# Two four-branch attention blocks in one kernel: latent projections regrouped by kind, stage boundaries done by token tiles, layer 1's memory keys made between the layers

## The chip, the cores and the metric

The kernel runs on one core of one Trainium2 chip. The metric is the device time of one execution in microseconds (us). Engines: TensorE (PE) with its weight loads (PEld), VectorE (DVE), ScalarE (ACT), GpSimd (POOL), SyncE (SP).

## The reference

One sequence of 512 tokens of width 1024 goes through two blocks of two layers each, all in float32.

A layer of the first block projects x by `w_in` into a latent query (384), a latent key and value (256), a rotated key (32), queries, keys and values of a stick-breaking and of a forgetting attention (256 each), four forget columns, memory queries (256), four gates (256 each) and a merge input (128). Each of four branches has four heads:

```python
q  = (rms(c_q) @ w_qb).reshape(b, s, 4, 96)        # 64 plain + 32 rotated
kv = (rms(c_kv) @ w_kvb).reshape(b, s, 4, 128)     # 64 key + 64 value
log_f = log_sigmoid(fox_f + fox_bias); c = cumsum(log_f)   # fox: logits + c[t] - c[s]
mk, mv = split(mem @ w_mem_kv)                      # mem has 256 rows
for n in range(4):
    yb = branches[n] * silu(gate_z[:, :, n])
    merged += sigmoid(merge_r @ w_merge_up)[:, :, n] * (yb @ w_branch[n])
x = layer_norm(ALPHA * x + merged @ w_out)
```

The branches are mla (causal, with the latents), sb (stick breaking), fox (causal with decay) and mem (over `mem`). A layer of the second block applies an rms norm, projects, runs four attentions A (dense), B (window), C (neighbourhood) and D (difference of two softmaxes), multiplies each by `silu` of a gate and adds the output projection to x. A last rms norm ends it.

## The kernel before, in words

**Precision.** Every projection is done in float32 by three matmuls of a rounded part (`xh`, `wh`) and a rest (`xl`, `wl`): lines 1338 to 1340, once for each of the contracted tiles of 128 (`k`). Weights come by DMA from SP into `wr`, two in flight, ScalarE rounds them (line 1480) and VectorE and GpSimd in turn subtract (lines 1805, 2245), 512 columns at a time; such a piece is a step `cast`. A projection lies "feature-major" (weights stationary, 512 tokens moving) or by token tiles (128 tokens stationary, 256 columns moving).

**Order.** `plan` (line 296) writes one list of steps, and each engine's program walks the same list and takes its own part, so the list fixes the order on each engine. All engines work strictly in that order; waits are on semaphores. Banks and buffers are taken and given back in the plan. In each attention stage `alongside` (line 528) interleaves the attention (main), the next branch's projections (fill) and the end of the branch before (tail), by modelled costs (`cost_of`, line 240; a lead of 5000 ns of fill, `LEAD`). `tick` (line 331) places one due cast, and in the beginning one step of the rope tables (`first_tables`, line 775), at fixed places between pieces of matmul. `wnext` takes the next weight and first lays down all of its casts that are still due.

**First block.** The features of x (transposes on PE, line 1297, rounding on ScalarE, rest on VectorE, line 1812) are made for all four token tiles. Then come the memory query, the gate of the memory branch and `project_mem` (line 606), which makes the memory keys and values of both layers; those of layer 1 are stored and loaded back later (`mkvstore`, `mkreload`). The stages are mem (filled by `mla_proj`, line 626), mla (filled by the sb projections and the split of the four forget columns), sb (filled by `fox_proj`, line 726: fox gate, forget columns, forget gate, fox projections) and fox (filled by three quarters of the merge). `mla_proj` makes the latents, their norms, four 96-wide query heads, each turned by its own rope step (line 1435; line 1921 copies it from the bank), four 64-wide key heads, the values and the gate. An mla logit is one matmul over 96 rows for each head. The forget gate is three functions on ScalarE, a sum along the tokens and eight copies on VectorE.

**Between layers.** The last quarter of the merge runs for eight tiles, each ends in a step `merged` (lines 1620, 1995). Output weights follow, four of 256 columns, each for four token tiles; the first matmul waits for merged tile 7 (`act_ready`, line 1231). With the last weight the norm of a token tile begins (`norm_x`: statistics, root on ScalarE, a Newton step, an Identity on ScalarE, the gain on VectorE, the bias on GpSimd, line 2280), then in layer 1 an rms norm, then the transposes of the next features. All features come before the next projection.

**Second block.** A's projections come alone; then stages A, B, D, C, filled by the next projections and by `out_partial` (line 931). Each query and key is turned by a `rope2` (line 1442) right behind its projection (`behind`, line 892). D's output is normed (line 1450). A gate takes two banks, a sigmoid each on ScalarE and a product each on VectorE (line 1891):

```python
held.append((yield from gemm("fm", w, 128 * c, 128 * c + 128, ("x", ep), range(8))))
...
put("gate", l=l, br=br, u=u, banks=held)
give(*held)
```

ScalarE's functions lie in table sets; a step whose function isn't in the set at hand gets a load ahead of it (`FUNCTIONS`, line 292).

Of the kernel before, what the change touches and what calls it, by code (L numbers as in the profile page):

```python
# [14 lines left out]
P = 128  # L15
S = 512
# [11 lines left out]
LEAD = 5000  # L28
# [6 lines left out]
def constants():  # L35
# [16 lines left out]
    col = np.zeros((P, 1), np.float32)  # L52
    col[64:96, 0] = np.concatenate([invf, invf])
    put("invf", col)
# [152 lines left out]


# [31 lines left out]
def cost_of(s):  # L240

    k = s.kind
    if k == "mm":
        n = s["n"] if s["mode"] in ("fm", "fox", "up", "br") else s["c1"] - s["c0"] if s["mode"] != "kvv" else 256
        return len(s["ks"]) * 3 * n * 0.451
# [15 lines left out]
def weights_in_order():  # L261

    out = []
    for l in range(2):
        for name, c0, n in (("mq", 2212, 256), ("g3", 3236, 256)):
            out.append((name, 8, n, l, c0))
        if l == 0:
            out += [(f"mkv{j}{n}", 8, 256, j, 256 * n) for j in (1, 0) for n in range(2)]
        out += [("cq0", 8, 256, l, 0), ("cq1", 8, 256, l, 256), ("ckr", 8, 160, l, 512), ("qb", 3, 384, l, 0),
                ("kvb", 2, 512, l, 0), ("g0", 8, 256, l, 2468)]  # L270
# [21 lines left out]
FUNCTIONS = {"gate": (GATES,), "sqk": (GATES,), "qk": (LOGS, TANHS), "dqk": (LOGS, TANHS), "mtanh": (TANHS,)}  # L292
# [3 lines left out]
def plan(known):  # L296
# [20 lines left out]
    st = {"i": 0, "split": 0, "load": 0}  # L317
# [37 lines left out]
    def pieces(ks, **at):  # L355
        for k in range(len(ks)):
            put("mm", ks=ks[k:k + 1], k0=ks[0], first=at["start"] and k == 0, last=k + 1 >= len(ks), done=False, **at)
# [5 lines left out]
    def gemm(mode, j, c0, c1, act, ks, n=S, tile=0, b=None, off=0, start=True):  # L363
        if b is None:
            b = GR[0].take()
        yield from pieces(ks, start=start, mode=mode, j=j, c0=c0, c1=c1, act=act, n=n, tile=tile, b=b, off=off)
        return b

# [21 lines left out]
    def gate(name, ep, br, l):  # L390
        w = wnext(name)
        held = []
        for c in range(2):
            held.append((yield from gemm("fm", w, 128 * c, 128 * c + 128, ("x", ep), range(8))))
            if c == 0:
                yield
        u = U.take()
        put("gate", l=l, br=br, u=u, banks=held)
        give(*held)
# [11 lines left out]
    def attention(l, br, front, finish):  # L411
# [60 lines left out]
        while later:  # L472
            yield 0
# [132 lines left out]
    def project_mem():  # L606
        for i in range(2):
            run(features("mem", i, X0))
        give(*X0)
        for j in (1, 0):  # L610
            for n in range(2):
                tm = TM.take() if j else None
                w = wnext(f"mkv{j}{n}")
                for c in range(2):
                    if n == 0:
                        b = drain(gemm("fm", w, 128 * c, 128 * c + 128, ("mem",), range(8), n=256))
                    else:
                        b = drain(gemm("tok", w, 0, 256, ("mem",), range(8), tile=c))
                    put("mkv", j=j, n=n, c=c, b=b, tm=tm)
                    give(b)  # L620
                wdone(w)
                if tm:
                    put("mkvstore", n=n, tm=tm)
                    give(tm)

    def mla_proj(l, box):
# [40 lines left out]
        b = yield from gemm("fm", w, 64, 160, ("x", l), range(8))  # L667
# [5 lines left out]
        yield  # L673
        w = wnext("qb")
        held = None
        for h in range(5):
            if h < 4:
                b = yield from gemm("fm", w, 96 * h, 96 * h + 96, ("nq", l), range(3))
                tm = TM.take()
                put("qb", l=l, h=h, b=b, tm=tm)  # L680
                give(b)
# [1763 lines left out]
```

## Time and profile before

| | |
|---|---|
| median of 3 runs | 1636.21 us (1634.75 to 1637.97) |
| profiled execution | 1632.88 us |
| its span, first to last instruction | 1631.1 us |
| mean granted TensorE clock | 0.950 of full |
| busy: PE, PEld, DVE, ACT, POOL | 1449.6, 1104.7, 924.1, 711.6, 370.7 us |

The span is the profiled execution without what lies around it, 1.8 us. Busy times of one engine are those of all its instructions, those that overlap counted once. A row of the timeline gives the start in us from the span's start, the length, and in brackets the idle time of the engine ahead of it with what ended it. L1338 is line 1338 of the kernel before.

### The profile page before, as it was taken

What the parts mean: (1) busy time and instruction counts of PE and PEld (TensorE: products, weight loads), DVE (VectorE), ACT (ScalarE), POOL (GpSimd) and SP (SyncE); (2) the same over time, 40 slices, a digit from 0 to 9 for tenths busy, and PEclk for the clock granted to TensorE, in tenths of its full rate; (3) what the DMA queues carried; (4) which work ended last, traced back from release to release, by engine and by line L of the source; (5) the groups of instructions that cost most, each with busy time, mean ns of one, the idle gap of its engine ahead of it and who ended that gap; (6) DMA issues with size and microseconds to landing.
All of it is one profiled execution on the core that took longest, in us unless ns stands there. A gap on an engine that the chain in (4) does not pass through costs nothing.

```text
span 1631.1 us, 21032 instructions
## 1 busy us (share of the span) xinstructions
PE 1449.6 (89%) x7904; PEld 1104.7 (68%) x7904; DVE 924.1 (57%) x1729; ACT 711.6 (44%) x1501; POOL 370.7 (23%) x269
## 2 busy tenths in 40 slices
PE   6898997999879989979989599998799799997897
PEld 5864784777867657757769466665578666664676
DVE  4547436556562563474674855467645565558555
ACT  2543544465333435444552535345333434445343
POOL 1313121245222221212461311320001111310001
PEclk8999998999989999989999699999899899998999
DMA  6552220124321121201254232521032423411221
GB/s 211 149 113 61 82 79 26 43 69 161 104 104 43 53 78 52 79 13 45 68 185 104 78 65 65 98 80 37 30 113 69 126 52 65 110 52 46 75 75 52
DMA packets 178152, 130.93 MB, mean 80 GB/s; under 512 B 76964, under 2 KB 167460, under 8 KB 178052
## 3 DMA queue, kind: packets, MB, share of 16 engines
q1 hardware_dynamic: 167126, 113.60, 24.2%
q10 hardware_dynamic: 10926, 15.99, 3.2%
q8 instruction: 63, 1.03, 0.3%
q14 instruction: 37, 0.30, 0.1%
HBM read 116.72 MB, written 12.85 MB: 79 GB/s over the span
## 4 chain that ended last, share of the span: by engine, by line
PE 72%; DVE 16%; ACT 6%; issue 3%; DMA 1%; ACTq 1%; SPq 0%; DVEq 0%
PE pb L1338 18%; PE pb L1339 17%; PE pb L1340 17%; PE pb L1362 6%; PE pb L1411 6%; PE pb L1389 4%; ACT prob L1467 2%; ACT tmp L1467 2%; DVE small L2078 1%; PE pb L1442 1%; DVE xl L1812 1%; DVE prob L2091 1%; PE pb L1373 1%; DVE scr L2100 1%; DMA wr<-w_out 1%
## 5 line engine op out<-in xcount | busy, mean ns | idle before, releaser
L2245 POOL TENSOR_TENSOR wl<-wr,wh 128x512 fp32r<-128x512 f32 x168 | 226.2, 1346 | 932.4 <-ACT wh L1480 927.5
L1338 PE MATMUL pb<-xh,wl 128*128 128x512 f32 (+1 forms) x784 | 339.8, 433 | 25.4 <-DVE wl L1805 9.2
L1339 PE MATMUL pb<-xl,wh 128*128 128x512 f32 (+1 forms) x784 | 312.0, 398 | 0.0
L1340 PE MATMUL pb<-xh,wh 128*128 128x512 f32 (+1 forms) x784 | 311.7, 398 | 0.0
L1480 ACT CAST wh<-wr 128x512 fp32r<-128x512 f32 x368 | 209.2, 600 | 116.0 <-PE pb L1340 76.4
L1805 DVE TENSOR_TENSOR wl<-wr,wh 128x512 fp32r<-128x512 f32 x200 | 156.5, 785 | 120.7 <-ACT wh L1480 119.9
L1338 PEld LDWEIGHTS pb<-xh,wl 128*128 128x128 f32 (+1 forms) x784 | 150.7, 192 | 99.1 <-issue 53.7
L1340 PEld LDWEIGHTS pb<-xh,wh 128*128 128x128 f32 (+1 forms) x784 | 150.2, 192 | 34.7
L1339 PEld LDWEIGHTS pb<-xl,wh 128*128 128x128 f32 (+1 forms) x784 | 151.1, 193 | 29.0 <-issue 3.8
L1389 PE MATMUL pb<-cst,prob 128*128 128x128 f32 x768 | 120.5, 278 | 37.8 <-DVE prob L2106 24.7
L1338 PE MATMUL pb<-wh,xl 128*128 128x256 f32 x448 | 133.6, 298 | 18.4 <-issue 12.9
L1389 PEld LDWEIGHTS pb<-cst,prob 128*128 128x128 f32 x768 | 94.8, 143 | 70.7 <-issue 33.7
L1339 PE MATMUL pb<-wl,xh 128*128 128x256 f32 x448 | 130.4, 291 | 0.0
L1340 PE MATMUL pb<-wh,xh 128*128 128x256 f32 x448 | 130.0, 290 | 0.0
L1467 ACT ACTIVATE prob<-prob,small 128x512 f32<-128x512 f32 (+3 forms) x128 | 76.3, 597 | 123.1 <-DVE small L2055 122.8
L1467 ACT ACTIVATE prob<-pb,small 128x512 f32<-128x512 f32 (+1 forms) x96 | 58.6, 613 | 136.3 <-DVE small L2042 86.3
L1467 ACT ACTIVATE tmp<-pb,cst 128x512 f32<-128x512 f32 (+3 forms) x116 | 74.5, 642 | 95.8 <-DVE tmp L2146 26.9
L1338 PEld LDWEIGHTS pb<-wh,xl 128*128 128x128 f32 x448 | 89.6, 200 | 21.9 <-issue 15.2
L2114 DVE COPY prob<-pb 128x512 f32<-128x512 f32 (+3 forms) x128 | 70.9, 554 | 46.4 <-PE pb L1389 45.1
L1699 ACT COPY prob<-pb 128x512 f32<-128x512 f32 (+3 forms) x128 | 61.2, 478 | 80.3 <-PE pb L1389 80.2
L1339 PEld LDWEIGHTS pb<-wl,xh 128*128 128x128 f32 x448 | 89.8, 200 | 1.0 <-issue 0.9
L1340 PEld LDWEIGHTS pb<-wh,xh 128*128 128x128 f32 x448 | 89.6, 200 | 0.0
(206 smaller groups left out, 2593.0 us busy)
## 6 DMA issues: line engine op xcount, KB each, us to landing
wr<-w_in SPq DMA_DIRECT2D x40, 1024.0 KB, 5.1
wr<-w_in SPq DMA_DIRECT2D x48, 256.0 KB, 4.5
wr<-w_out SPq DMA_DIRECT2D x10, 1024.0 KB, 5.1
wr<-w_branch SPq DMA_DIRECT2D x48, 128.0 KB, 2.3
x<-prob SPq DMA_DIRECT2D x12, 512.0 KB, 2.6
wr<-w_out SPq DMA_DIRECT2D x48, 128.0 KB, 2.9
wr<-w_mem_kv SPq DMA_DIRECT2D x4, 1024.0 KB, 9.9
prob<-x ACTq DMA_DIRECT2D x2, 2048.0 KB, 8.0
```

Of the source, the lines that this page charges most:

```text
L1338: e.matmul(ps, ll, rh, start=start, stop=False)
L1339: e.matmul(ps, lh, rl, start=False, stop=False)
L1340: t = e.matmul(ps, lh, rh, start=False, stop=stop)
L1362: t = e.matmul(bank(b)[:, 0:128 * (hi - lo)], lhs, rhs, start=True, stop=True)
L1389: t = e.transpose(bank(b)[:, c], probs(p)[:, c], C("ident"))
L1411: t = e.matmul(bank(b)[64 * half:64 * half + 64, lo:hi], v_[:, j, vc:vc + 64], turns(s["t"][half])[:, j, lo - 256 * ih:hi - 256 * ih], sta ...
L1467: return e.activation(o, i, f, bias=C("zero", 0, i.shape[0]) if bias is None else bias, scale=scale, **kw)
L1480: e.copy(wh[:, j % 2, c0:c1], wr[:, j % 2, c0:c1]).then_inc(w_hi.sem, w_hi.mark((j, c)))
L1699: t = e.copy(turns(t_)[:, lo:hi, 128 * i:128 * i + 128], bank(b)[:, 0:128 * (hi - lo)].rearrange("p (j c) -> p j c", c=128))
L1805: t = e.tensor_tensor(wl[:, j % 2, c0:c1], wr[:, j % 2, c0:c1], wh[:, j % 2, c0:c1].bitcast(F32), ALU.subtract)
L2114: t = e.tensor_copy(turns(t_)[:, lo:hi, 128 * i:128 * i + 128], bank(b)[:, 0:128 * (hi - lo)].rearrange("p (j c) -> p j c", c=128))
L2245: t = e.tensor_tensor(wl[:, j % 2, c0:c1], wr[:, j % 2, c0:c1], wh[:, j % 2, c0:c1].bitcast(F32), ALU.subtract)
```

## The change

- The weights `ckr`, `qb` and `kvb` are loaded in narrow pieces that put columns of a kind together: the latent's last tile, then the forget columns twice beside the rotated key twice; the plain parts of the four heads in two tiles, the rotated parts in one; keys in two tiles, then values. The forget columns' own weights, matmuls and buffers go. Positions are turned once for the key and once for all four query heads. A logit is two matmuls, over 64 plain and over 32 rotated rows.
- The forget gate moves from the sb stage to the end of `mla_proj`, its copies between the fox projections; the mla gate moves ahead of the queries.
- Gates use tanh of half the input, one bank at a time; the factor 1/2 goes into later products.
- `project_mem` makes one layer's memory keys; layer 1's are made behind the last output weights of layer 0 from a second load of `mem`.
- Output weights: the first begins with six of eight merged tiles for four token tiles, the last two are taken together token tile by token tile, with the norm's steps (now two products on VectorE with mean and root) and the next features between them; casts are held back meanwhile.
- The first projection (layer 0's memory query, A's gate) is done for 256 tokens, then the other two token tiles' features, then the other 256.
- In A and B and D `behind` waits three pieces; `out_partial` starts with four of six inputs for two tiles, ahead of the end of the D stage's tail; `LEAD` is 4500. At the start, x and mem are issued from ScalarE's queue and the rope tables begin behind the memory query.

```diff
-LEAD = 5000
+LEAD = 4500
...
-FUNCTIONS = {"gate": (GATES,), "sqk": (GATES,), "qk": (LOGS, TANHS), "dqk": (LOGS, TANHS), "mtanh": (TANHS,)}
+FUNCTIONS = {"gate": (TANHS, GATES), "sqk": (GATES,), "qk": (LOGS, TANHS), "dqk": (LOGS, TANHS), "mtanh": (TANHS, GATES)}
...
-        if due:
+        if due and not st["hold"]:
...
+    def opened(w, ep, between):
+
+        held = [GR[0].take() for _ in range(2)]
+        for half in range(2):
+            for c in range(2):
+                drain(gemm("fm", w, 128 * c, 128 * c + 128, ("x", ep), range(8), n=256, b=held[c], off=256 * half,
+                           end=half == 1))
+            if not half:
+                between()
+        return held
...
-        b = yield from gemm("fm", w, 64, 160, ("x", l), range(8))
+        b = yield from gemm("fm", w, 128, 256, ("x", l), range(8))
         put("krope", l=l, b=b)
...
         w = wnext("qb")
...
+        for c in range(2):
+            b = yield from gemm("fm", w, 128 * c, 128 * c + 128, ("nq", l), range(3))
+            put("qnope", l=l, c=c, b=b)
             give(b)
             tick()
             yield
...
+        turn_rope("k", None)
+        yield
+        w = wnext("kvb")
+        for c in range(2):
+            b = yield from gemm("fm", w, 128 * c, 128 * c + 128, ("nkv", l), range(2))
+            put("knope", l=l, c=c, b=b)
...
+        turn_rope("q", tm)
...
         wdone(w)
-        for x in gate("g0", l, "mla", l):
-            if x is not None:
-                box["u"] = x
-            yield
+        e_ = TM.take()
+        put("foxgate", l=l, e=e_)
+        give(e_)
...
-        b = yield from gemm("fox", -1, 0, 36, ("x", l), range(8))
...
+        w = wnext("wo")
+        held = [drain(gemm("tok", w, 0, 256, ("m", l), range(6), tile=i, end=False, stop=False)) for i in range(4)]
+        for i in range(4):
+            out_tile(0, i, drain(gemm("tok", w, 0, 256, ("m", l), (6, 7), tile=i, b=held[i], start=False)))
...
+        pair = [wnext("wo") for _ in range(2)]
+        st["hold"], late = True, []
+        for i in range(4):
+            for m in (2, 3):
+                b = drain(gemm("tok", pair[m - 2], 0, 256, ("m", l), range(8), tile=i))
+                advance_late(late)
+                out_tile(m, i, b)
...
+            parts = mem_parts(1)
+            for turned in ((0, 1), (2,), (3,), ()):
+                next(parts)
+                advance_late(late)
+                for i in turned:
+                    run(features(1, i, (X[i],)))
...
         def behind(n, tm, sq):
+            for _ in range(3):
+                yield
...
+        at = {"ckr": [(0, 512, 128), (128, 2208, 32), (160, 2208, 32), (192, 640, 32), (224, 640, 32)],
+              "qb": [(64 * h, 96 * h, 64) for h in range(4)] + [(256 + 32 * h, 96 * h + 64, 32) for h in range(4)],
+              "kvb": [(64 * h + 256 * r, 128 * h + 64 * r, 64) for r in range(2) for h in range(4)]}
...
+                if br == "mla":
+                    for half, b in enumerate(s["b"]):
+                        r = slice(64 + 32 * half, 96 + 32 * half)
+                        t = e.matmul(bank(b)[:, 0:128 * (hi - lo)], q_rope[r, c, ti], k_rope[r, tk], start=False, stop=True,
+                                     tile_position=(64 + 32 * half, 0))
...
-                    w.wait_ge(a_fn, a_fn.at(("lnapplied", l, i)))
-                    w.wait_ge(d_res, d_res.at(("ln", l)))
-                    e.tensor_tensor(x, x, lnp[:, 0, :], ALU.mult).then_inc(v_fn.sem, v_fn.mark(("lngain", l, i)))
...
+                t = e.scalar_tensor_tensor(x, x, 1.0, bank(b), ALU.add, ALU.mult)
+                t.then_inc(v_fn.sem, v_fn.mark(("gate", s["u"], c), ends=(b,)))
```

## Rows read from the trace of the kernel before

**Rows 1.** The page: busy time; the chain that ended last.
```profile
PE 1449.6 (89%) x7904; PEld 1104.7 (68%) x7904; DVE 924.1 (57%) x1729; ACT 711.6 (44%) x1501; POOL 370.7 (23%) x269
...
PE 72%; DVE 16%; ACT 6%; issue 3%; DMA 1%; ACTq 1%; SPq 0%; DVEq 0%
```

**Rows 2.** Stretches: length, busy us of PE, PEld, DVE, ACT, POOL; PEclk, DMA.
```profile
11.30:20.60 9.30, 0.10 (x2) 0.09 (x1) 5.99 (x9) 5.07 (x10) 5.27 (x4) 0.65 0.51 122
133.90:144.30 10.40, 4.67 (x16) 2.05 (x17) 10.27 (x15) 2.78 (x9) 4.57 (x3) 0.81 0.01 2
266.80:277.30 10.50, 1.21 (x6) 0.82 (x6) 10.19 (x17) 2.37 (x7) 1.40 (x1) 0.66 0.00 0
415.20:421.70 6.50, 0.10 (x2) 0.05 (x1) 6.30 (x9) 3.70 (x7) 3.17 (x2) 0.89 0.11 32
470.30:490.60 20.30, 7.09 (x34) 5.62 (x33) 17.99 (x27) 8.76 (x16) 7.01 (x3) 0.61 0.27 107
907.10:933.80 26.70, 7.92 (x34) 6.32 (x33) 25.47 (x47) 16.21 (x32) 7.02 (x3) 0.59 0.20 81
1273.50:1287.30 13.80, 5.12 (x26) 4.07 (x25) 13.33 (x25) 10.39 (x23) 2.38 (x2) 0.63 0.43 153
961.10:979.30 18.20, 14.37 (x55) 9.86 (x55) 14.78 (x22) 7.03 (x12) 2.60 (x2) 1.00 0.29 59
1114.80:1118.50 3.70, 0.17 (x2) 0.09 (x1) 1.52 (x3) 3.39 (x5) 1.26 (x1) 1.00 0.06 12
1175.90:1195.00 19.10, 13.15 (x80) 10.91 (x79) 10.43 (x18) 4.97 (x8) 1.27 (x1) 0.82 0.44 152
```

**Rows 3.** The same columns, sum of the 18 stretches at half clock.
```profile
sum 162.90, PE 94.25 PEld 72.21 DVE 119.29 ACT 65.76 POOL 38.28; mean PE 5.24 PEld 4.01 DVE 6.63 ACT 3.65 POOL 2.13
```

**Rows 4.** PE's timeline: start, length, line, operation, tiles, shapes.
```profile
24.44 0.40 PE L1338 MATMUL pb<-xh,wl 128*128 128x512 f32 x1
...
43.96 0.39 PE L1340 MATMUL pb<-xh,wh 128*128 128x512 f32 x1
...
903.01 0.28 PE L1338 MATMUL pb<-wh,xl 128*128 128x256 f32 x1
...
903.37 0.28 PE L1338 MATMUL pb<-wh,xl 128*128 128x256 f32 x1
```

**Rows 5.** PE's groups by line and form (count, busy us, mean ns, idle before).
```profile
L1338 PE MATMUL pb<-xh,fwl 128*36 128x512 f32 x16 | 6.5, 405 | 0.0
...
L1338 PE MATMUL pb<-yh,wl 128*64 128x512 f32 x16 | 7.7, 483 | 0.0
...
L1338 PE MATMUL pb<-yh,wl 128*96 128x512 f32 x24 | 11.1, 463 | 1.9 <-DVE tmp L1930 1.5 <-issue 0.4
...
L1435 PE MATMUL pb<-tmp,cst 96*96 96x512 f32 x16 | 9.9, 700 | 7.4 <-DVE tmp L1921 7.4
```

**Rows 6.** PE's timeline: logits over 96 rows, and over 32.
```profile
216.40 1.98 PE L1362 MATMUL pb<-setA 96*128 96x512 f32 x4
...
1105.28 1.14 PE L1373 MATMUL pb<-setA 32*128 32x512 f32 x8
1106.35 0.50 PE L1338 MATMUL pb<-xh,wl 128*128 128x512 f32 x1
1106.69 0.40 PE L1339 MATMUL pb<-xl,wh 128*128 128x512 f32 x1
```

**Rows 7.** Timelines of PE at the start and ScalarE in the stick-breaking stage.
```profile
20.54 0.77 PE L1338 MATMUL pb<-xh,wl 128*128 128x512 f32 x1 [9.20 <-DVE wl L1805]
...
263.00 2.23 ACT L1467 ACTIVATE tmp<-tmp,cst 36x512 f32<-36x512 f32 x3
```

**Rows 8.** PE's groups: the transposes of probabilities.
```profile
L1389 PE MATMUL pb<-cst,prob 128*128 128x128 f32 x768 | 120.5, 278 | 37.8 <-DVE prob L2106 24.7 <-ACT prob L1467 11.9 <-DVE scr L2124 1.2
```

**Rows 9.** DMA issues: queue, count, KB each, median us to landing.
```profile
wr<-w_in SPq DMA_DIRECT2D x48, 256.0 KB, 4.5
...
tmp<-w_in SPq DMA_DIRECT2D x4, 16.0 KB, 3.8
```

More of the change, by code:

```diff
@@ L353, in wdone, with pieces @@
         last.a["done"] = True
-    def pieces(ks, **at):
+    def pieces(ks, end, stop, **at):
         for k in range(len(ks)):
-            put("mm", ks=ks[k:k + 1], k0=ks[0], first=at["start"] and k == 0, last=k + 1 >= len(ks), done=False, **at)
+            over = k + 1 >= len(ks)
+            put("mm", ks=ks[k:k + 1], k0=ks[0], first=at["start"] and k == 0, last=end and over, stop=stop and over,
+                done=False, **at)
             if k + 1 < len(ks):
@@ L361, in pieces, with gemm, advance_late @@
                 yield
-    def gemm(mode, j, c0, c1, act, ks, n=S, tile=0, b=None, off=0, start=True):
+    def gemm(mode, j, c0, c1, act, ks, n=S, tile=0, b=None, off=0, start=True, end=True, stop=True):
         if b is None:
             b = GR[0].take()
-        yield from pieces(ks, start=start, mode=mode, j=j, c0=c0, c1=c1, act=act, n=n, tile=tile, b=b, off=off)
+        yield from pieces(ks, end, stop, start=start, mode=mode, j=j, c0=c0, c1=c1, act=act, n=n, tile=tile, b=b, off=off)
         return b
+    def advance_late(late):
+        return [g for g in late if next(g, g) is not g]
+    def opened(w, ep, between):
[7 more added lines that the diff above has]
+        return held
     def drain(g):
@@ L472, in attention @@
         while later:
-            yield 0
+            yield now() + 2500
             advance()
@@ L779, in first_tables @@
                 yield
-    aside.append(first_tables())
     for l in range(2):
-        run(proj_fm("mq", l, "mem", "q", l, False))
+        w = wnext("mq")
+        if l:
+            held = [drain(gemm("fm", w, 128 * c, 128 * c + 128, ("x", l), range(8))) for c in range(2)]
+        else:
+            held = opened(w, l, lambda: last_features(l, *X))
+        wdone(w)
+        for c in range(2):
+            put("head", l=l, br="mem", part="q", c=c, b=held[c], wide=False)
+        give(*held)
+        if l == 0:
+            aside.append(first_tables())
         u = run(gate("g3", l, "mem", l))
         if l == 0:
-            project_mem()
+            mem_features(0)
+            rest_of(mem_parts(0))
             put("lambdas")
@@ new lines, in plan @@
+        st["hold"] = False
+        if l:
+            for i in range(2):
+                advance_late(late)
+                run(features(2, i))
+            while advance_late(late):
+                pass
+            give(*X, *X0)
+        else:
+            parts = mem_parts(1)
+            for turned in ((0, 1), (2,), (3,), ()):
+                next(parts)
+                advance_late(late)
+                for i in turned:
+                    run(features(1, i, (X[i],)))
+            rest_of(parts)
+            give(*X)
@@ L929, in project, with out_partial @@
         yield
-    def out_partial(l):
+    def out_partial(l, before):
         for m in range(4):
             w = wnext("wo2a")
+            held = {}
+            if m == 0:
+                for i in range(2):
+                    held[i] = yield from gemm("tok", w, 0, 256, ("y2", l), range(4), tile=i, end=False, stop=False)
+                rest_of(before)
             for i in range(4):
-                b = yield from gemm("tok", w, 0, 256, ("y2", l), range(6), tile=i)
+                b = yield from gemm("tok", w, 0, 256, ("y2", l), range(4 if i in held else 0, 6), tile=i, b=held.get(i),
+                                    start=i not in held)
                 put("acc", l=l, m=m, i=i, b=b)
```

553 lines of the change are left out of this document (241 added, 312 removed).

## The prediction

> **What bounds the kernel now.** I read five views, in this order. First the page: TensorE (PE) is busy for 89% of the span, and 72% of the chain that ended last is PE's own work, 16% VectorE's, 6% ScalarE's [rows 1]. The kernel is bound by its matmuls and, where they stop, by short chains on VectorE and ScalarE. So two kinds of edit pay: fewer matmuls, and work for PE in the holes. The holes are 1631.1 - 1449.6 = 181.5 us. Second, the busy time by stretch, for where they are [rows 2]: idle is a row's length less its PE busy time. The ten stretches hold 84.6 us of it, and four of them (turns, forget gate, merge, A) and the two of D return once more, at about the same length, in the other layer of their block: with those repeats 119 us. Third, the granted clock: in 18 stretches, nearly all behind such a hole, PE ran at the lower of its two levels (1.2 instead of 2.4 GHz) while it was busy for 94.25 us [rows 3]; half of that, 47 us, is a second price of the holes. Fourth, PE's timeline for what a matmul costs: between [rows 4]'s first two rows lie 86 steps of 512 columns in 19.52 us, 0.227 each; three of 256 columns take 0.36 in the last two, 0.120 each. I count by these distances, since busy times overlap. Fifth, the groups by form, for how many matmuls go [rows 5].
>
> The profiled execution took 1632.9 us (span 1631.1 and 1.8 around it), 3.3 below the median of 1636.2. I sum changes on that execution and take them off the median. A difference under 0.2% (3 us) is about what a measurement of this kernel can't tell from none.
>
> **Matmuls.** The forget columns now ride in the unused columns of the position-key tile: 3 x 16 = 48 matmuls of 36 columns go, 48 x 0.227 = 10.9 us. The queries take three 128-wide tiles instead of four 96-wide ones: 72 become 54, 4.1 us. The keys take two full tiles instead of four half ones: 48 become 24, 5.4 us. Ten turns of positions become four; the row shows 9.9 us for eight of them, tails included, so I take 0.9 each, 5.3 us. Together 25.7 [rows 5, 4]. Added: the 16 transposes of the memory a second time (the 32 of the boundary are 7.09 us at the lower clock [rows 2], so 1.8 here), and three projections cut into token halves, 96 x 0.120 - 48 x 0.227 = 0.6 each, 1.8. Then the logits of mla: one group over 96 rows becomes a 64-row pair and a 32-row pair. The trace has no such sequence. The old group of four at 512 keys is busy for 1.98 us; eight 32-row matmuls on four row groups, the nearest row, are for 1.14, so if two groups share the array as four do, two pairs are 2.28 at most, 0.3 a step [rows 6]. With no sharing the old 1.98 is paid twice: 2560 columns a layer, 9.9 us, so +20 in both. I take the nearest row less half for the shorter steps, 0.2 a step, 16 steps, +3 (0 to +20). Net **-19**, bounds -22 and -2.
> The Trainium skill (TensorEngine Tiling, Key Properties) speaks against this edit: changing the tiling mode drains the engine, and the new step changes it once more. The row shows what that is worth: behind the 32-row group the follower's next matmul starts 0.34 us after it instead of 0.23 [rows 6], so a change of mode is worth 0.1 us; by the rule 16 more of them are some 2 us and the sum 2 higher, by my rows they are in the 3. No run here shows the new sequence.
>
> **Holes.** *Start*, 9.2 us [rows 2]: VectorE works in order, and the rope tables, which wait for the positions' DMA, stand ahead of the first weight's low part; that part then holds PE [rows 7]. The tables move behind the first projection, x is issued from ScalarE's queue instead of ahead of the weights on SP's, and the first half starts on two feature tiles. ScalarE issues five DMAs first; that is hidden until x lands. The other half waits for two more tiles' casts, some 2 us. -6 (0 to -9). *Turns*, 5.7 us twice: copy, turn and four adds of VectorE run between matmuls that need them; now the gate lies ahead and the turn of q comes after the keys. VectorE gets the position-key copies in exchange. -9 (0 to -11). *Forget gate*, 9.3 us twice: in the stick-breaking stage ScalarE does 2.23 us of logarithms between two table loads, and VectorE waits for it with the sticks queued behind [rows 7]. It moves to the end of the mem stage, whose functions share its table. VectorE still waits there, with mem's maxima behind it: 2 us each left. -15 (-5 to -19). *Merge to output*, 6.4 us twice: the first output matmul waits for all eight merged tiles. Now it asks for its own, and six of eight for four token tiles are 72 x 0.120 = 8.6 us of cover. -11 (-6 to -13). *Layer 0 to 1*, 13.2 us: the last two output weights are done token tile by token tile, so three of the four norm chains run under matmuls; behind the last stand layer 1's memory keys and values, 96 x 0.120 = 11.5 us, taken from the start of the kernel. GpSimd's adds in the norm go. -12 (-5 to -13). *Layer 1 to block two*, 18.8 us: the same, but the cover is only half a gate projection, 5.8 us, and VectorE still owes two tiles' norm. -9 (0 to -12). *Between block two's layers*, 8.7: -5 (0 to -7). *Turns in A*, 3.8 us twice: three pieces later. -6 (0 to -8). *D*, 3.7 and 6.0 us twice: the gate of C needs a table load ahead of its two sigmoids while both projection banks are held; the tanh shares the table of the exponentials and each bank goes back alone. At D's end the last square's wait gets partial output sums ahead of it. -11 (-4 to -16).
> Holding back casts during the paired output weights could make the second of them late: its cast waits for the weight two before, and 2.9 us of matmuls (24 x 0.120) lie ahead. Under 1 us, four times at most; costed at nothing. ScalarE loses some fifteen table loads, but is no bound: nothing.
> *Clock*: of the 94.25 us, two in three lie behind holes that I shrink; I take -20 (-8 to -32), as the shrunk holes may still lower it.
>
> Holes and clock are -104. What is late next are the chains of the attention steps, which stay: transposes today wait 37.8 us for probabilities [rows 8]. I let a sixth of the 104 come back, 17. Sum: -19 - 104 + 17 = **-106**, so 1636.2 - 106 = **1530**.
>
> **Rivals.** *A. The waits move.* The steps are planned ahead with modelled costs; a chain that is shorter in one place is waited for in another. For: VectorE is busy for 17.99 of 20.3 us and 25.47 of 26.7 at two boundaries [rows 2], so it has little room to run ahead. Then half of the 104 stays: 1636.2 - 19 - 52 = 1565. A boundary whose fill doesn't run, because transposes of an unfinished tile stand ahead of it on PE, gives about the same (three boundaries and their clock, some 33 less gained).
> *B. Late weights.* ckr, qb and kvb are loaded in 5, 8 and 8 narrow pieces. If each narrow piece took the 3.8 us of the forget weights' load, 1,024 short runs, one behind the other [rows 9], qb needed 30 us against 96 x 0.227 = 21.8 us of matmuls ahead of it and kvb 30 against 17: late by 22 us a layer, 44 in all, 1574. Against: four 64-column pieces of one weight land in 4.5 us each, side by side.
> The Trainium skill (DMA: Bandwidth & Descriptors, Specifications) asks for 512 bytes a descriptor at full rate; the 64-column pieces are 256 bytes, the 32-column ones 128. By the row of 4.5 us the halved size costs nothing that this kernel waits for; by the rule these loads would come nearer to B.
> *C. Attention becomes the bound, and it is slower.* The shortened projections are the cover of 128 attention steps (16 stages of 8). If the exposed wait of a step grows by more than 106 / 128 = 0.83 us, all is lost; at 1.2 us it is 1530 + 154 = 1684. Against: all transposes of a kind wait 37.8 us now, 0.3 a step, and only 26 us of cover go, all in mem's and mla's stages and the first gate's.
>
> **How the numbers follow.** Forecast 0.57, A 0.26, B 0.11, C 0.04, no change 0.02. The forecast's own bounds reach 1474 and 1605 if every term is at its end, which they won't be together; 1490 leaves most of the low side in, 1585 takes in A and B. Faster 0.94, same 0.02, slower 0.04.
>
> **What would show it.** PE 1395 to 1425 us busy, idle near 110, 90 to 110 us at the lower clock instead of 163, some 22 table loads; no forget matmuls; no 7 us wait in the stick-breaking stage; under 3 us of idle between layers 0 and 1 and 8 to 11 between layer 1 and block two. Wrong would be: idle above 140 (A), PE waiting for weights in the mem stage (B), transposes that wait over 100 us in all (C), or mla logits over 2.6 us a step at 512 keys.

## The result, and the profile after

The changed kernel takes **1551.69 us** (median of 4 runs, 1550.07 to 1553.37), against 1636.65 in the four runs beside it (one more than in the table ahead): a ratio of 0.9482, interval 0.9465 to 0.9499. So 85 us were gained where 106 were forecast; 1551.69 lies inside the range of 1490 to 1585, and the sign was right. The profiled execution took 1553.30 (span 1551.2), 79.6 less than the profiled one of before. I account for these 79.6; the rest is that one execution lay below its median and the other above. One of the four runs of experiment 6 took 2312.69 us at a mean granted clock of 0.558 and is left out there.

Page of the changed kernel, the busy times of [rows 1]:

```profile
PE 1418.2 (91%) x8026; PEld 1092.2 (70%) x8026; DVE 903.9 (58%) x1705; ACT 682.7 (44%) x1478; POOL 367.7 (24%) x265
```

The sum over its 15 stretches at the lower clock, the columns of [rows 3]:

```profile
sum 83.03, PE 58.36 PEld 42.12 DVE 53.17 ACT 29.35 POOL 9.20; mean PE 3.89 PEld 2.81 DVE 3.54 ACT 1.96 POOL 0.61
```

Idle time of PE is 1551.2 - 1418.2 = 133.0, 48.5 less than before. Busy time is 31.4 less. Of that the clock has (94.25 - 58.36) / 2 = 18.0, and the matmuls the other 13.4. Together 79.9, the difference of the spans.

Stretches of the changed kernel, the columns of [rows 2]; the second row is a hole that [rows 2] doesn't have, and the row at 1050.3 is D's step at the gate of C, as the row at 1114.8 was:

```profile
9.40:16.00 6.60, 0.12 (x2) 0.07 (x1) 1.96 (x3) 2.11 (x4) 0.24 (x1) 1.00 1.05 377
73.80:78.80 5.00, 0.02 (x2) 0.01 (x1) 1.69 (x4) 1.77 (x5) 1.06 (x1) 0.91 0.92 189
119.40:127.40 8.00, 4.18 (x23) 3.15 (x22) 6.77 (x13) 4.21 (x11) 3.75 (x3) 1.00 0.29 66
...
259.60:262.00 2.40, 0.04 (x3) 0.04 (x2) 1.54 (x3) 2.24 (x6) 1.27 (x1) 1.00 0.00 0
386.80:389.10 2.30, 0.68 (x4) 0.47 (x4) 2.30 (x4) 0.54 (x1) 1.01 (x2) 1.00 0.21 68
445.90:453.80 7.90, 2.16 (x14) 1.65 (x14) 7.60 (x13) 3.04 (x7) 3.16 (x2) 0.97 0.47 136
846.40:875.80 29.40, 12.62 (x82) 11.74 (x80) 24.40 (x43) 15.38 (x32) 6.55 (x4) 0.77 0.29 99
906.50:913.70 7.20, 5.39 (x21) 3.34 (x20) 5.77 (x9) 4.74 (x8) 1.50 (x2) 1.00 0.00 0
...
1050.30:1053.90 3.60, 0.04 (x5) 0.05 (x4) 2.12 (x5) 2.59 (x6) 1.27 (x1) 1.00 0.00 0
1106.40:1129.00 22.60, 19.91 (x155) 17.78 (x154) 13.62 (x21) 7.36 (x13) 1.27 (x1) 1.00 0.53 163
1197.30:1221.30 24.00, 12.06 (x81) 11.35 (x80) 15.40 (x29) 11.84 (x23) 5.76 (x4) 0.79 0.56 154
```

The merge, the stick-breaking stage and D lost most of their idle time, the turns over a third. The two boundaries that lead to a block-two layer (846 and 1197) together lost nothing: 16.8 and 11.9 us of idle time where 18.8 and 8.7 were. Term by term, the waits of PE of over 0.5 us summed over both traces (each stage with all its waits; the clock's -18.0 is that of this pair of executions):

| term | forecast | traces |
|---|---|---|
| matmuls | -19 | -13.4 |
| start | -6 | -0.3 |
| turns of block one | -9 | -4.5 |
| forget gate | -15 | -11.5 |
| merge to output | -11 | -13.7 |
| layer 0 to 1 | -12 | -7.7 |
| layer 1 to block two | -9 | -2.0 |
| between block two's layers | -5 | +3.3 |
| turns in A | -6 | -1.7 |
| D | -11 | -12.5 |
| clock | -20 | -18.0 |
| comes back elsewhere | +17 | +2.3 (mem's first step) |

### The profile page after: what moved, and what is told of

Its sections match the earlier page's. It is cut to its first block, busy times and chain, and to the rows that moved or that the text cites. A ratio compares the mean times of both kernels' runs of the same rounds, so it can differ in the third digit from the quotient of the medians.

```text
span 1551.2 us, 21240 instructions
## 1 busy us (share of the span) xinstructions
PE 1418.2 (91%) x8026; PEld 1092.2 (70%) x8026; DVE 903.9 (58%) x1705; ACT 682.7 (44%) x1478; POOL 367.7 (24%) x265
## 4 chain that ended last, share of the span: by engine, by line
PE 69%; DVE 18%; ACT 8%; issue 3%; DMA 1%; ACTq 1%; POOL 0%; DVEq 0%; SPq 0%; POOLq 0%
PE pb L1390 18%; PE pb L1391 16%; PE pb L1392 16%; PE pb L1468 6%; PE pb L1412 5%; PE pb L1446 4%; ACT prob L1524 2%; ACT wh L1542 2%; ACT tmp L1524 1%; DVE wl L1851 1%; DVE small L2116 1%; DVE xl L1858 1%; PE pb L1430 1%; DVE scr L2138 1%; DMA wr<-w_in 1%
## 5 line engine op out<-in xcount | busy, mean ns | idle before, releaser
L2283 POOL TENSOR_TENSOR wl<-wr,wh 128x512 fp32r<-128x512 f32 x170 | 237.2, 1395 | 896.8 <-ACT wh L1542 893.0
L1390 PE MATMUL pb<-xh,wl 128*128 128x512 f32 (+1 forms) x832 | 352.2, 423 | 29.2 <-DVE xl L1858 21.7
L1391 PE MATMUL pb<-xl,wh 128*128 128x512 f32 (+1 forms) x832 | 322.6, 388 | 0.0
L1392 PE MATMUL pb<-xh,wh 128*128 128x512 f32 (+1 forms) x832 | 322.0, 387 | 0.0
L1851 DVE TENSOR_TENSOR wl<-wr,wh 128x512 fp32r<-128x512 f32 x200 | 164.0, 821 | 164.6 <-ACT wh L1542 164.3
L1390 PEld LDWEIGHTS pb<-xh,wl 128*128 128x128 f32 x832 | 162.4, 195 | 110.0 <-issue 60.1
L1392 PEld LDWEIGHTS pb<-xh,wh 128*128 128x128 f32 x832 | 162.4, 195 | 31.9
L1391 PEld LDWEIGHTS pb<-xl,wh 128*128 128x128 f32 x832 | 163.3, 196 | 24.2 <-issue 3.8
L1446 PE MATMUL pb<-cst,prob 128*128 128x128 f32 x768 | 118.9, 276 | 23.9 <-ACT prob L1524 13.1
L1390 PE MATMUL pb<-wh,yl 128*128 128x256 f32 (+1 forms) x272 | 86.7, 319 | 2.5 <-DVE wl L1851 1.3
L1391 PEld LDWEIGHTS pb<-wl,xh 128*128 128x128 f32 x448 | 85.8, 192 | 0.7 <-issue 0.5
```

Source lines behind the costliest of these rows:

```text
L1390: e.matmul(ps, ll, rh, start=start, stop=False)
L1391: e.matmul(ps, lh, rl, start=False, stop=False)
L1392: t = e.matmul(ps, lh, rh, start=False, stop=stop)
L1446: t = e.transpose(bank(b)[:, c], probs(p)[:, c], C("ident"))
L1851: t = e.tensor_tensor(wl[:, j % 2, c0:c1], wr[:, j % 2, c0:c1], wh[:, j % 2, c0:c1].bitcast(F32), ALU.subtract)
L2283: t = e.tensor_tensor(wl[:, j % 2, c0:c1], wr[:, j % 2, c0:c1], wh[:, j % 2, c0:c1].bitcast(F32), ALU.subtract)
```

## Experiments

Each kernel is the changed one with the edit shown, and is compared with 1551.7 of the changed kernel; the ratios are to the kernel before, run beside it.

**1. The transposes of the last tiles earlier.** The first projection of a block runs in two token halves, with the other two tiles' transposes between them.

```
-            if not half:
-                between()
+                if half == 0 and c == 0:
+                    between()
```

> The transposes of token tiles 2 and 3 go after the first 24 of the first half's 48 matmuls, at all three places with token halves; nothing else changes. Changed kernel: 1551.7. Theory (TensorE's order: the transposes stand behind the half gate, so that their casts and differences have no cover): between the block-two layers the data of tile 3 is there at 1208.2 and the half gate starts only at 1209.45, so the wait of 1.88 at 1219.42 and the 1.9 of bare transposes go, and 1.9 to 2.3 at the start; between layer 1 and block two tile 3 is ready only at 870.0, in the middle of the half gate, so 1 or 2 of 4.16 there. Sum -5 to -8: 1544 to 1547. Rival (VectorE's chain is the bound at all three places, whatever the order): the transposes wait in their new place, 1550 to 1553.

Measured: 1547.01, ratio 0.9460 (0.9441 to 0.9479). First the changed kernel, PE's timeline at the boundaries (the bracket is the idle time before and what ended it), and VectorE's before the second half:

```profile
869.92 3.43 DVE L1851 TENSOR_TENSOR wl<-wr,wh 128x512 fp32r<-128x512 f32 x2
873.27 2.47 DVE L1858 TENSOR_TENSOR xl<-pb,xh 128x512 fp32r<-128x512 f32 x4
...
875.79 0.39 PE L1390 MATMUL pb<-xh,wl 128*128 128x256 f32 x1 [4.16 <-DVE xl L1858]
...
1209.45 0.58 PE L1390 MATMUL pb<-xh,wl 128*128 128x256 f32 x1 [8.36 <-DVE xl L1858]
1221.30 0.39 PE L1390 MATMUL pb<-xh,wl 128*128 128x256 f32 x1 [1.88 <-DVE xl L1858]
```

Then the edited kernel, PE's timeline at the boundary to block two:

```profile
857.96 0.58 PE L1390 MATMUL pb<-xh,wl 128*128 128x256 f32 x1 [5.42 <-DVE xl L1858]
866.07 1.97 PE L1353 MATMUL pb<-cst,setB 128*128 128x128 f32 x8 [2.10 <-DVE setB L2068]
```

The waits ahead of the second halves at the start and between block two's layers are gone, and the 4.16 has become one of 2.10 for the norm itself. So part of these boundaries' idle time was the order on PE. The 5.42 and 8.36 ahead of the first half stay.

**2. No halves in block two.**

```
-        for x in gate(br + "g", ep, br, l, (lambda: last_features(ep)) if br == "A" else None):
+        if br == "A":
+            last_features(ep)
+        for x in gate(br + "g", ep, br, l):
```

> The first gate of both block-two layers is made in one piece again, after all four token tiles are turned; the first projection of layer 0 keeps its halves. Theory (the halves gain nothing here because the second half is late by about as much as the first is early): 48 matmuls of 256 columns, 5.8 us of work, come off 29.3 us between the end of the output matmuls and the start of the second half in one place and 24.0 us in the other, which leaves 23.5 and 18.2; without halves I count 27 and 15. Net within 3 us of 1551.7: 1549 to 1555. Rival (the halves hide some 5 us at each boundary, as the prediction had it): 1560 or more.

Measured: 1552.00 (1547.13 to 1555.25), ratio 0.9488 (0.9462 to 0.9514). The halves as the change has them gain nothing that can be told. The trace of this run shows why: without them PE waits 7.18 + 7.44 + 4.12 + 1.45 = 20.2 us ahead of block two, where the changed kernel waits 16.8, and 1.69 + 2.92 + 2.27 + 1.67 = 8.6 between block two's layers, where it waits 11.9. So the halves save 3.4 us at the one boundary and lose 3.4 at the other, where the earlier first half is paid with a late second half.

**3. mem loaded later.**

```
 (begin, ScalarE's queue)
-                t = e.dma_start(memt, ...)
-                t.then_inc(d_mem.sem, d_mem.mark("mem0"))
 (cast)
+                if (j, c) == (0, 3):
+                    t = e.dma_start(memt, ...)
+                    t.then_inc(d_mem.sem, d_mem.mark("mem0"))
```

> The load of mem (1 MB) is issued by ScalarE after the casts of the first weight load, not at the program's start. Changed kernel: 1551.7. Theory (the start gained nothing because x and mem, 3 MB on ScalarE's queue, run beside the first weights on SyncE's, which land at 14.45 against 12.13 before): the weights land near 12, the first matmul comes 1.5 to 2.5 earlier: 1549 to 1550.5. Rival (the second half of the weights, at 17.25, or mem itself, then late for its transposes at 46, sets the pace): 1551 to 1554.

Measured: 1549.22, ratio 0.9472 (0.9448 to 0.9497); from the times alone that can't be told from the changed kernel, so the trace has to carry it. The DMA issues (median us to landing) up to 30 us and the first projection, of the changed kernel:

```profile
wr<-w_in SPq DMA_DIRECT2D x2, 1024.0 KB, 14.4
...
15.96 0.55 PE L1390 MATMUL pb<-xh,wl 128*128 128x256 f32 x1 [6.48 <-DVE wl L1851]
```

and of the edited one:

```profile
wr<-w_in SPq DMA_DIRECT2D x2, 1024.0 KB, 11.7
...
13.10 0.55 PE L1390 MATMUL pb<-xh,wl 128*128 128x256 f32 x1 [3.74 <-DVE wl L1852]
```

In the kernel before, the weights stood behind x on one queue and landed 9.1 us after their issue, at 12.13. In the changed one they are issued 1.9 earlier and land at 14.45, because mem's 1 MB shares the way with them. The first projection comes 2.86 earlier without it. Even so ScalarE can round the first weights only at 11.61, about 0.5 before the old 12.15.

**4. The forget chain back in its old place.**

```
 (end of mla_proj)
-        e_ = TM.take()
-        put("foxgate", l=l, e=e_)
-        give(e_)
 (fox_proj, behind put("zeros"))
+        e_ = TM.take()
+        put("foxgate", l=l, e=e_)
+        give(e_)
```

> The forget chain (three activations, a difference and the running sum) goes back to the stick-breaking stage, behind the gate g2, where it was before; the forget columns stay in ckr's tile and the row writes stay where the change has them. Theory (the hole of 7.1 and 2.2 us was that chain in the queues ahead of the attention's work, so its place decides): 5 to 9 us a layer come back with some lower clock, 1562 to 1572. Rival (the hole came from the separate forget matmuls and from writing the four rows in one go, which both stay away here): 1550 to 1555.

Measured: 1568.73, ratio 0.9593 (0.9566 to 0.9620), 17 us slower. Timeline of the edited kernel in the stick-breaking stage:

```profile
237.87 0.72 ACT L1524 ACTIVATE tmp<-fz,cst 36x512 f32<-36x512 f32 x1
...
240.85 1.22 DVE L1999 TENSOR_TENSOR_SCAN fz<-tmp 36x512 f32<-36x512 f32 x1
...
243.63 0.66 PE L1446 MATMUL pb<-cst,prob 128*128 128x128 f32 x2 [6.05 <-DVE prob L2144]
```

The hole is back (6.05 here, 6.06 in layer 1): the chain in front of the sticks made it. Idle time rose by 8.4 us (1566.1 - 1424.7 = 141.4), and the busy time at the lower clock from 58.36 to 70.43, another 6.0. Not all of that lies behind the hole. The stretches that do are, in the columns of [rows 2],

```profile
240.06:250.30 10.24, 5.90 (x17) 3.96 (x19) 9.76 (x19) 4.46 (x9) 0.00 (x0) 0.50 0.00 0
...
659.90:670.14 10.24, 6.28 (x21) 4.19 (x21) 9.49 (x19) 4.09 (x7) 0.00 (x0) 0.50 0.01 2
```

where the changed kernel has nothing in the first place and 3.41 us busy in the second: 8.8 more, worth 4.4.

**5. The gates' table loads back.**

```
-FUNCTIONS = {"gate": (TANHS, GATES), ...
+FUNCTIONS = {"gate": (GATES,), ...
```

> The gates' tanh is taken from the table set that holds the sigmoid, so that ScalarE loads a table for each gate and another back after it, as before the change; the values are the same. Prediction: the some fifteen table loads fewer (13 in the traces, of 1.28 us) cost nothing, since ScalarE is no bound: 1550 to 1553. Rival (each load stands ahead of an exponential that TensorE waits for): 13 x 1.28 = 17 at most, 1556 to 1569.

Measured: 1563.25, ratio 0.9565 (0.9542 to 0.9588). ScalarE's group of table loads (count, busy us, mean ns, idle before) and a wait in D, first of the changed kernel:

```profile
L1536 ACT ACT_TABLE_LOAD x26 | 33.4, 1283 | 0.5
...
1053.88 1.95 PE L1430 MATMUL pb<-setA 32*128 32x512 f32 x8 [3.56 <-DVE prob L2152]
```

and of the edited one:

```profile
L1536 ACT ACT_TABLE_LOAD x56 | 71.8, 1283 | 1.0
...
1059.53 2.09 PE L1430 MATMUL pb<-setA 32*128 32x512 f32 x8 [5.78 <-DVE prob L2152]
```

The edit made 30 more loads, not the 13 by which the traces of before and after differ, so it overshoots the undoing. But loads are not free: 11.6 / 30 = 0.39 us each, of which D's two waits show 2 x 2.2. For 13 of them that is some 5 us, an estimate.

**6. Turns of block two at once.**

```
-            for _ in range(3):
-                yield
             b, t2 = GR[0].take(), TM.take()
```

> The three steps by which a rope turn of block two is put off behind the next projection's matmuls are taken out again; nothing else. Changed kernel: 1551.7. Theory (the turn stands on TensorE ahead of VectorE's result if it comes at once, as the waits of 1.54 and 1.52 per layer did before): 2 to 4 us a layer come back, 1555 to 1560. Rival (those waits were shortened by the other parts, and the delay only moves what waits): 1550 to 1553.

Measured: 1559.64 (median of 1554.03, 1559.64 and 1561.23), ratio 0.9526 (0.9491 to 0.9561). PE's timeline in A, and the sum of the 18 stretches at the lower clock:

```profile
898.47 1.12 PE L1497 MATMUL pb<-tmp,cst 128*128 128x512 f32 x2 [1.55 <-DVE tmp L2182]
...
sum 96.37, PE 69.15 PEld 51.58 DVE 58.25 ACT 35.89 POOL 15.25; mean PE 3.84 PEld 2.87 DVE 3.24 ACT 1.99 POOL 0.85
```

This wait and a second one of 1.52 are those of before, and the other layer has them again. In both layers the turns of A wait 4.0 us more than in the changed kernel, so the delay is what shortened them; all idle time is 2.8 more (1557.6 - 1421.8 = 135.8). What that costs in time is less sure, since the interval overlaps that of the changed kernel (0.9465 to 0.9499). The 69.15 - 58.36 = 10.8 us more busy at the lower clock aren't shown to come from it: the new stretches are at 12.84, 125.48 and 238.12, in block one, where the edit changes nothing, and at 1224.57, ahead of the turns, and none stands behind those turns. The clock also differs between executions of this one kernel: 1554.03 us at a mean of 0.976, 1559.64 at 0.970.

**7. The bias spread from SyncE.** At 73.8 PE waits 4.98 us in mem's first step; before it was 2.70 there.

```
 (scalar_program)
-            elif k == "spread":
...
 (sync_program, the same lines at the same step)
+            elif k == "spread":
...
```

> The two DMAs that spread the position bias (each 60 x 64 rows) are issued by SyncE at the same step, not by ScalarE. Theory (ScalarE's queue is held for 1.44 and 7.45 us by the issue alone, from 67.43 to 76.36, with the first exponentials of the mem stage behind it, so TensorE waits 4.98 us at 73.81 and then runs 6.8 us at half clock): the wait goes and most of the clock's loss of about 2.7: 1544 to 1547. SyncE has nothing due between its loads at 67.4 and 83.2. Rival (what waits there waits for the weights or the reductions anyway, or the held SyncE is late with a load): 1550 to 1556.

Measured: 1546.52, ratio 0.9456 (0.9436 to 0.9477). Timeline of the changed kernel (ACTq is ScalarE issuing a DMA):

```profile
67.43 1.44 ACTq L1567 DMA_DIRECT2D zscr<-setA  x1
68.91 7.45 ACTq L1567 DMA_DIRECT2D zscr<-setA  x1
...
78.79 0.48 PE L1446 MATMUL pb<-cst,prob 128*128 128x128 f32 x1 [4.98 <-ACT prob L1524]
```

and of the edited one:

```profile
67.68 9.38 SPq L2366 DMA_DIRECT2D zscr<-setA  x2
...
72.74 0.38 PE L1446 MATMUL pb<-cst,prob 128*128 128x128 f32 x2
```

The issue alone held ScalarE's queue for 8.9 us, with casts and exponentials behind it; ScalarE stood idle for 6.40 us. On SyncE it takes 9.38 and PE waits for nothing behind it. The hole is gone. The issue isn't new. In the kernel before it was

```profile
77.46 9.59 ACTq L1503 DMA_DIRECT2D zscr<-setA  x2
```

and PE waited 2.70 us behind it. The change exposed more of it.

**8. Layer 1's memory keys after its first projection and gate.**

```
 (out of mla, layer 0)
-            mem_features(1)
-            parts = mem_parts(1)  ... next(parts) ... rest_of(parts)
 (layer 1, behind gate g3)
+            mem_features(1)
+            rest_of(mem_parts(1))
```

> Layer 1's memory keys and values (96 matmuls of 256 columns, 11.5 us at full clock, and 16 transposes) are made after layer 1's first projection and gate, as in layer 0, not between the output projection of layer 0 and that projection. Theory (they fill the wait for the last tiles' norms): idle time between the layers goes from 5.6 to 13 or more, with some lower clock: +8 to +13, 1559 to 1565. Rival (the chains alone have become short enough, and the fill only changes places with the wait): 1550 to 1555.

Measured: 1567.05, ratio 0.9580 (0.9553 to 0.9607), 15.4 slower. PE's timeline of the edited kernel between the layers:

```profile
436.55 1.90 PE L1351 MATMUL pb<-cst,prob 128*128 128x128 f32 x8 [4.33 <-DVE prob L2058]
...
444.77 1.97 PE L1351 MATMUL pb<-cst,prob 128*128 128x128 f32 x8 [6.32 <-DVE prob L2058]
448.19 0.77 PE L1388 MATMUL pb<-xh,wl 128*128 128x512 f32 x1 [1.45 <-DVE xl L1856]
```

4.33 + 6.32 + 1.45 = 12.1 us idle where the changed kernel has 5.6, and another 2.20 ahead of the keys in their new place, and 9.29 us busy at the lower clock at this boundary instead of 3.05. What made this boundary short is the fill: without it the wait is near the 13.2 of before.

**9. Output columns one after the other.**

```
-        pair = [wnext("wo") for _ in range(2)]
-        st["hold"], late = True, []
-        for i in range(4):
-            for m in (2, 3):
...
+        late = []
+        for m in (2, 3):
+            w = wnext("wo")
+            for i in range(4):
...
```

> The last two column blocks of w_out are made one after the other again, each over all four token tiles, without the hold of the weight casts; the first block's 4 + 2 split and the chains stay. Theory (with the pair a token tile is complete every 5.8 us and VectorE's chain begins 17 us before the last matmul; without it, 8.6 us before it): both boundaries get longer, the one between the layers by 3 to 9 (the keys cover some), the one to block two by 6 to 9: 1560 to 1569. Rival (VectorE's work sets the end either way, or the held casts cost as much): 1549 to 1555.

Measured: 1550.46, ratio 0.9487 (0.9460 to 0.9513): no difference. PE's timeline of the edited kernel at both boundaries:

```profile
445.54 1.56 PE L1348 MATMUL pb<-cst,prob 128*128 128x128 f32 x8 [2.24 <-DVE prob L2055]
...
849.93 1.97 PE L1348 MATMUL pb<-cst,setB 128*128 128x128 f32 x8 [7.58 <-DVE stats L1819]
...
856.37 1.97 PE L1348 MATMUL pb<-cst,setB 128*128 128x128 f32 x8 [4.47 <-DVE stats L1819]
```

Between the layers the wait for the last tile is shorter than with the pair (2.24 against 4.25), and at block two the first half begins 17.4 us after the last output matmul instead of 15.5, but its second half comes at about the same time (29.7 against 29.4); PE's waits there are 7.58 + 4.47 + 1.40 + 1.88 = 15.3 against 16.8. My theory, that the pair carried both boundaries, falls; the rival holds. It named two causes, that VectorE's work sets the end either way or that the held casts cost as much as the pair gains, and as the edit takes out both the pair and the hold, it doesn't tell them apart.

**10. Early output matmuls in D taken out.**

```
             if m == 0:
-                for i in range(2):
-                    held[i] = yield from gemm("tok", w, 0, 256, ("y2", l), range(4), ...)
                 rest_of(before)
```

> The first output matmuls of block two, for two token tiles by four of six blocks, no longer come ahead of the end of the D attention; all come after it, as before. Theory (they cover D's last corrections, whose waits fell from 5.95 to 2.6 us a layer): 3 to 5 us a layer come back, 1557 to 1562. Rival (the waits fell because the corrections are spaced further apart, and the early matmuls only change places): 1550 to 1554.

Measured: 1551.42, ratio 0.9495 (0.9465 to 0.9526). PE's timeline at D's end, edited kernel:

```profile
1108.07 0.38 PE L1390 MATMUL pb<-wh,xl 128*128 128x256 f32 x1 [1.61 <-DVE tmp L1820]
```

The wait is the 1.61 of the changed kernel, so the early matmuls are not what shortened D's end. Nor is the delay of the turns, since experiment 6 has the same 1.64 and 0.52 there. What is left of the change there is the wider spacing of the corrections; that was not tried alone.

**11. Three edits together, and 12. with the casts held.** The edits of 1, 3 and 7; then also

```
 (opened)
+        st["hold"] = True
...
                 if half == 0 and c == 0:
                     between()
+                    st["hold"] = False
 (end of mla_proj)
-        st["hold"] = False
+        st["hold"] = bool(l)
...
+            st["hold"] = False
```

> The three edits that each gained on the changed kernel, together: transposes of the last tiles after 24 matmuls (-4.7 alone), mem's load after the first weights (-2.5), the bias spread from SyncE (-5.2). Theory (three places, no shared cover, so they add): 1551.7 - 12.4 = 1539, 1537 to 1542. Rival (the planned steps behind them wait for what came earlier, and a third or more comes back): 1543 to 1547.

> As the three together, and the weight casts are held from the first half of a gate with halves until the last two token tiles are turned. Theory (at the boundary to block two, two differences of weights, 3.35 us on VectorE from 870.00, stand ahead of the splits of the last tiles, which end the wait): 2 to 3.5 less than the three alone, 1536 to 1538. Rival (the next weights, cast later, are then late behind the gate): 1539 to 1543.

Measured: 1540.28 (ratio 0.9415, 0.9390 to 0.9441) and 1537.23 (0.9397, 0.9375 to 0.9419). The three add up: 11.4 of 12.4. Their interval lies below that of the changed kernel, so this version beats both. The hold is not shown to be worth anything. With it PE waits 5.42 and 2.22 us at the boundary to block two, without it 5.42 and 2.18: the weights' differences had stopped being what PE waits for once the transposes came earlier. Nor did the rival's late weights appear. The 3 us between the medians are within their intervals.

## Why the prediction was right or wrong

**Right.** That PE's matmuls and its holes bound the kernel, and that the lower clock is a second price: terms of -13.4, -48.5 and -18.0 in the traces, all with the forecast's sign. The forget gate's cause (by experiment 4 its place alone brings back 8.4 us of idle time and with its clock 17 us), its size (-11.5 for -15), the merge (-13.7 for -11) and the clock (-18.0 for -20) came out near. The merge was not undone alone, so its cause is read from the traces: the wait of 6.40 at its end is gone. Busy time is inside the 1395 to 1425 named, no forget matmuls are left, and the 7-us wait is gone. Rival B is out: no wait of PE over 0.5 us in the mem stage is for qb or kvb. Their narrow pieces land as

```profile
wr<-mla_w_kvb SPq DMA_DIRECT2D x8, 64.0 KB, 2.0
wr<-mla_w_qb SPq DMA_DIRECT2D x4, 96.0 KB, 2.5
wr<-mla_w_qb SPq DMA_DIRECT2D x4, 48.0 KB, 2.2
```

(DMA issues of 95 to 130 us), less than the 3.8 that B put on each. Rival C is out too: all transposes of probabilities wait 23.9 us, less than before. Rival A had named idle time over 140; it is 133.0 where the forecast had some 110, so the time lies between the two. Of the other signs, 83 us at the lower clock are fewer than the 90 to 110 named, 29 table loads are more than 22 (before there were 42, so the fifteen fewer of the sum would have been 27), and the idle times between layers 0 and 1 (5.6, not under 3) and ahead of block two (16.8, not 8 to 11) are the ones that failed.

**Wrong: the boundaries into block two** (15 us of the gap). "Layer 1 to block two: the same, but the cover is only half a gate projection", -9 (0 to -12), and -5 (0 to -7) between block two's layers. I counted the half gate as cover and nothing for what the cut costs. The traces show -2.0, inside its bounds, and +3.3, outside. Ahead of the first half stand 12.6 and 10.0 us of idle, in which VectorE still works; behind it the last tiles' transposes, casts and differences had no cover. Experiments 1 and 2 show this: the halves as built are worth nothing, 3.4 saved at one boundary and lost at the other, in a better order some 4.7 with the start. What stays is, by the trace, the norm's work on VectorE, busy for 24.40 of 29.40 us in the stretch at 846; no run shortens that work alone.

**Wrong: the start**, -6 (0 to -9), was -0.3. The step took x off the weights' queue and called ScalarE's five issues "hidden until x lands"; it left out that the fifth of them, mem, then shares the bandwidth with the weights. By experiment 3 that is 2.9 us in the trace. The second half's wait of 1.9 was in the step, as some 2. The rest of this miss stays open. The Trainium skill (DMA: Bandwidth & Descriptors, Issuing engines are not separate DMA queues) says that DMAs from all issuing engines run on the same 16 DMA engines, so that another queue saves only the time of issuing. The landings above agree. It also calls that issuing time usually small beside the DMA; the 7.45 us that ScalarE was held in experiment 7 is the exception here, beside a median of 18.5 us to landing for the two DMAs.

**Wrong in size.** *Layer 0 to 1*: -7.7 for -12. The mechanism I named first, chains under the paired output matmuls, is worth nothing (experiment 9); the fill is worth 15.4 with its clock (experiment 8). *Turns in A*: the turns' waits fell from 3.8 a layer to 1.8 and 1.9, but 1.36 a layer is new at A's first logits, so -1.2 for -6 (the table's -1.7 leaves out one wait of 0.50). *Turns of block one*: -4.5 for -9; the turn's own wait of 3.71 went, and a product with the values in the mem stage now waits 3.1 in its place, where it waited 1.3 and 1.9. *Matmuls*: the logits of mla cost more than the +3 taken. By PE's groups, the 96-row ones were busy for 7.9 + 5.8 + 4.1 + 2.4 = 20.2 us, the 64-row and 32-row ones that replace them for 26.0, so +5.8. By distances, as the forecast counts, it is more. A full step of 512 keys, first of the kernel before, behind the row at 216.40 of [rows 6],

```profile
217.81 0.80 PE L1338 MATMUL pb<-xh,wl 128*128 128x512 f32 x1
218.45 0.40 PE L1339 MATMUL pb<-xl,wh 128*128 128x512 f32 x1
```

then of the changed kernel, with two matmuls of a projection behind transposes:

```profile
199.59 1.13 PE L1412 MATMUL pb<-setA 64*128 64x512 f32 x4
200.65 1.13 PE L1418 MATMUL pb<-setA 32*128 32x512 f32 x4
201.71 0.50 PE L1390 MATMUL pb<-xh,wl 128*128 128x512 f32 x1
202.05 0.40 PE L1391 MATMUL pb<-xl,wh 128*128 128x512 f32 x1
...
205.14 0.48 PE L1390 MATMUL pb<-xh,wl 128*128 128x512 f32 x1
205.45 0.40 PE L1391 MATMUL pb<-xl,wh 128*128 128x512 f32 x1
```

The logits are busy for 2.19 at 512 keys, near the 2.28 that bounded them, and below the 2.6 that would have been wrong. But from their start to that of the second matmul behind them it is 202.05 - 199.59 = 2.46 us, against 218.45 - 216.40 = 2.05, and in the same way 0.50, 0.50 and 0.49 more at 128, 256 and 384 keys: +7.6 in 16 steps, almost 0.5 a step and not 0.2. The Trainium skill (TensorEngine Tiling (Array Packing), Key Properties) has the engine drain at a change of tiling mode. No run here shows what that costs: behind the 32-row group the first two matmuls are 0.34 apart instead of 0.23, but behind transposes, which use the whole array as they do, 0.31 (205.14 to 205.45), so the 0.1 that I read as the change of mode is nearly all there without one. Another 1 us of the matmul term I can't assign.

**Wrong and unnoticed in the sum.** "ScalarE loses some fifteen table loads, but is no bound: nothing." By experiment 5 a load costs 0.39 us on average. D's size (-12.5 for -11) is luck, since neither part that I named carried it. The partial output sums at its end cost nothing to take away (experiment 10). And at the gate of C the kernel before waited 3.5 us (the 3.7 of the sum is the length of its row):

```profile
1118.41 0.50 PE L1338 MATMUL pb<-xh,wl 128*128 128x512 f32 x1 [3.54 <-DVE u L1891]
```

The changed one waits 3.56 there, now ahead of D's next logits (the row at 1053.88 in experiment 5). What fell are the waits around these two places, for causes that stay open. Of the 17 us that I let come back, 2.3 stands in the table (mem's first step, behind ScalarE's issue of two DMAs); another 3.0 at mem's products with the values, 2.7 at A's first logits and 1.2 at the merge's first matmuls stand inside the other terms. With these the terms were smaller by 41 in all. So the 17 us stood in for sizes that I had too large, and without them the forecast would have been 123 us where 85 came: that it came as near as it did is partly luck.

## What to carry to other kernels

A cut that lets half of the work start early pays only if what the other half needs comes, in each engine's order, under the first half; look at the queue behind the cut, not at the cover alone. Price a long hole twice: in experiment 4 the clock behind the two holes cost 4.4 us on top of the waiting. Short waits like those of experiment 6 had no such stretch behind them. Of several edits aimed at one boundary, one may do all the work (the fill), and another none (the pair): undo each alone before keeping it.

## What the hardware showed that I had not expected

ScalarE's queue was held for 1.44 and 7.45 us by issuing two DMAs of 60 x 64 rows each; SyncE took 9.38 for the same two. Such an issue belongs on a queue with nothing behind it. And loads of 3 MB on one queue moved the landing of the 1 MB load issued on the other by 2.3 us past where it was with all of them on one queue and mem last, although it was issued 1.9 us earlier. With the 1 MB of mem taken out of the 3 it came 2.9 us sooner (experiment 3).
